# Local attention: own and context keys on two halves of the partitions, three pairs of sum banks, an aligned expert loop

## What is computed

```python
s_win = jnp.einsum('bqhgd,bkhd->bhgqk', qb, kb).astype(jnp.float32) * scale
s_win = jnp.where(valid, s_win, NEG_INF)
s_ctx = jnp.einsum('bqhgd,bkhd->bhgqk', qb, kc).astype(jnp.float32) * scale
...
p = jax.nn.softmax(jnp.concatenate([s_win, s_ctx, s_sink], axis=-1), axis=-1).astype(q.dtype)
```

## Time and profile before

| | |
|---|---|
| median of three executions | 2874.34 us |
| the profiled execution's own time | 2875.95 us |
| its span in the trace | 2874.1 us |
| PE busy | 2626.2 us (91%) |
| DVE busy | 1074.2 us (37%) |
| ACT busy | 706.6 us (25%) |
| granted TensorE clock, mean | 0.964 |

### The profile page before, as it was taken

One profiled execution on the slowest core, in us unless ns is written; L12 is line 12 of the kernel. 1 busy time (PEld: TensorE's weight loads), 2 busy tenths in 40 slices (PEclk: granted clock), 3 DMA queues, 4 the chain that ended last, 5 costly groups with the idle time before them and its releaser, 6 DMA issues. The chain is left out here.

```text
span 2874.1 us, 43176 instructions
## 1 busy us (share of the span) xinstructions
PE 2626.2 (91%) x17318; PEld 1387.9 (48%) x17318; DVE 1074.2 (37%) x2323; ACT 706.6 (25%) x1843; POOL 220.2 (8%) x258
## 2 busy tenths in 40 slices
PE   7999999999998899998799999997899969999987
PEld 3565654564645666655344444435566543332222
DVE  3023341123345665456222121236652562333224
ACT  2134321234322245323111121213342321000000
POOL 1100200000101001012000000001100010000000
PEclk9999999999998999999899999998999979999999
DMA  7244515342714001114899999972102239999996
GB/s 222 81 128 109 155 66 132 103 127 72 186 47 118 8 1 43 66 44 189 331 394 396 399 401 397 403 217 62 28 1 96 96 143 361 410 406 411 411 409 262
DMA packets 268621, 569.96 MB, mean 198 GB/s; under 512 B 12416, under 2 KB 203200, under 8 KB 219328
## 3 DMA queue, kind: packets, MB, share of 16 engines
q1 hardware_dynamic: 256512, 528.69, 50.2%
q0 software_dynamic: 11824, 39.18, 5.0%
q10 hardware_dynamic: 144, 0.14, 0.0%
HBM read 551.53 MB, written 16.42 MB: 198 GB/s over the span
## 5 line engine op out<-in xcount | busy, mean ns | idle before, releaser
L459 PE MATMUL ps<-turned,ring 128*128 128x512 f32 (+1 forms) x1408 | 553.0, 553 | 11.7 <-ACT turned L1605 8.8
L459 PEld LDWEIGHTS ps<-turned,ring 128*128 128x128 f32 x1408 | 271.3, 194 | 282.1 <-issue 262.6
L707 PE MATMUL ps<-ring,mixT 128*128 128x512 f32 x512 | 225.3, 597 | 0.8 <-DVE mixT L1821 0.8
L1260 ACT ACTIVATE work<-ps 128x512 f32<-128x512 f32 x32 | 19.1, 598 | 684.4 <-PE ps L1164 404.5
L505 PE MATMUL ps<-kz,qz 96*128 96x256 f32 (+3 forms) x384 | 164.7, 516 | 23.8 <-DVE qz L2243 8.8
L1849 ACT ACTIVATE probs_v<-ps,col 128x256 f32<-128x256 f32 (+5 forms) x216 | 136.4, 632 | 70.0 <-DVE col L1799 34.7
L1862 ACT ACTIVATE probsT<-ps 128x512 f32<-128x512 f32 (+3 forms) x280 | 120.2, 455 | 134.6 <-PE ps L545 105.9
L707 PEld LDWEIGHTS ps<-ring,mixT 128*128 128x128 f32 x512 | 96.4, 191 | 115.7 <-issue 114.5
L470 PE MATMUL ps<-ring,turned 128*128 128x128 f32 x1216 | 140.3, 278 | 4.5 <-ACT turned L1605 4.5
L1795 DVE TENSOR_REDUCE col<-ps 128x1 f32<-128x256 f32 (+4 forms) x136 | 78.8, 579 | 174.3 <-PE ps L505 168.0
L470 PEld LDWEIGHTS ps<-ring,turned 128*128 128x128 f32 x1216 | 140.0, 195 | 7.9 <-ACT turned L1605 4.8
(11 more groups left out here) (309 smaller groups left out, 3550.3 us busy)
## 6 DMA issues: line engine op xcount, KB each, us to landing
ring<-in_w_gate SPq DMA_DIRECT2D x64, 1024.0 KB, 19.8
mixT<-in_w_up SPq DMA_DIRECT2D x64, 1024.0 KB, 13.5
ring<-in_w_mod SPq DMA_DIRECT2D x96, 512.0 KB, 4.0
ring<-in_w_up SPq DMA_DIRECT2D x48, 1024.0 KB
ring<-in_w_in SPq DMA_DIRECT2D x82, 512.0 KB, 7.2
turned<-in_w_gate SPq DMA_DIRECT2D x32, 1024.0 KB
mixcT<-in_w_down SPq DMA_DIRECT2D x32, 1024.0 KB
probs_v<-in_w_down SPq DMA_DIRECT2D x32, 1024.0 KB
```

The costliest lines, as they stand in the source:

```text
L459: mm = nc.tensor.matmul(ps[:, b, 0:n], w[:, k, :], rhs[:, k, 0:n], start=(k == 0), stop=(k == KD - 1))
L707: mm = nc.tensor.matmul(ps[:, b, :], lhs[:, k, tl * P:(tl + 1) * P], w, start=(k == 0), stop=(k == KD - 1))
```

## The change

- Queries of the window attention are held twice, on partitions 0 to 63 and, by a new ACT copy (`act_queries_twice`, one of 64 x 1024 per query chunk, two per part), on 64 to 127. The window's own keys stay on 0 to 63, its context keys move to 64 to 127 (`act_ctx_keys`, and `act_heads` for `aq` into `QC`). The scores are then a matmul on each half, own keys and all 256 context keys in one; every other score of the second stack (`ca`, `nb`, `cb`) reads 64 partitions instead of 96. PE's first score of a part waits for the copy (`queries_twice`).
- `score_span` places the own scores at the end of the first bank, the context's at the start of the second. POOL's four memsets per layer go.
- `sum_banks` gives layer 0 three pairs of banks, so that only tile 3 waits (for tile 0); the four multiplications of the context's share move on DVE behind the first tile's centring (`dve_gate_context`); `pe_combine_context` waits for tile 2's centring instead of tile 3's.
- PE's expert loop begins at slot 0 of a fetch block.

```diff
--- before.py
+++ after.py
@@ -417,7 +417,15 @@
         def score_span(u):
 
             o = (seq[u] % 2) * 1024 if wide(u[0]) else (seq[u] % 4) * 512
+            if wide(u[0]):
+
+                o += SEQ - (keys_of(u) - NC) * P
             return o, o + keys_of(u) * P
+
+        def score_banks(u):
+
+            o, end = score_span(u)
+            return o // 512 * 512, -(-end // 512) * 512
 
         def probs_span(u):
 
@@ -475,31 +483,33 @@
 
         def pe_scores(pe, u):
             (kind, l, part), t, hh = u
-            w = before(u, score_span)
+            w = before(u, score_banks)
             if w is not None:
 
                 pe.wait_ge(*at("probs", w))
             S = s_psum(u)
-            q = (QC if kind in ("ca", "cb") else qz)[0:KROWS, hh, t * P:(t + 1) * P]
+            q = qz[0:KROWS, hh, t * P:(t + 1) * P]
+            own, other = slice(0, HD), slice(HD, P)
             parts = []
             if kind in ("fox", "mla"):
                 parts = [(q, kz[0:KROWS, hh, 0:(t + 1) * P], 0), (unit16, causal16, t * P)]
             elif kind == "mem":
                 parts = [(q, kz[0:KROWS, hh, 0:CTX], 0)]
             elif kind in ("ca", "cb"):
-                parts = [(q, KC[0:KROWS, part if kind == "ca" else 2 + hh, :], 0)]
+                R, keys = (other, part) if kind == "ca" else (own, 2 + hh)
+                parts = [(QC[R, hh, t * P:(t + 1) * P], KC[R, keys, :], 0)]
             elif kind == "nb":
-                parts = [(q, kz[0:KROWS, hh, :], 0), (q, KC[0:KROWS, 2 + hh, :], SEQ)]
+                parts = [(q[own, :], kz[own, hh, :], 0), (q[own, :], KC[own, 2 + hh, :], SEQ)]
             else:
                 j0, j1 = max(t - 1, 0), min(t + 1, NT - 1)
                 w = (j1 - j0 + 1) * P
-                parts = [(q, kz[0:KROWS, part, j0 * P:(j1 + 1) * P], 0)]
+                parts = [(qz[own, hh, t * P:(t + 1) * P], kz[own, part, j0 * P:(j1 + 1) * P], 0),
+                         (qz[other, hh, t * P:(t + 1) * P], KC[other, part, :], w)]
                 if t > 0:
                     parts.append((unit16, before16, 0))
                 if t < NT - 1:
 
                     parts.append((unit16, causal16, w - P))
-                parts += [(q, KC[0:KROWS, part, c * P:(c + 1) * P], w + c * P) for c in range(NC)]
             for lhs, rhs, o in parts:
 
                 mm = nc.tensor.matmul(S[:, o:o + rhs.shape[-1]], lhs, rhs, start=lhs is not unit16, stop=True,
@@ -945,8 +955,7 @@
                     if l == 0:
                         pe_conv_stat(pe, l, 1, "cvar")
                     q_job(3)
-                pe.wait_ge(*at("roped", (l, "aq", 2 * part + 1)))
-                pe.wait_ge(*at("zero_rows", ("second", l)))
+                pe.wait_ge(*at("queries_twice", (l, 2 * part + 1)))
                 if l == 0:
                     pe.wait_ge(*emptied(("aq", l, 2 * part + 1, 1)))
                 pe.wait_ge(*emptied(("bv", l, 1, 1)))
@@ -1069,9 +1078,11 @@
 
         def pairs_of_rounds(eng, body, first=2, last=EXPERTS - 2):
 
+
+            head = {eng.engine: 0} if eng.engine == mybir.EngineType.PE else None
             for e in range(first):
                 body(e, e % 2)
-            with eng.Fori(first, last, 2) as i:
+            with nc.Fori(first, last, 2, engines=[eng.engine], head_slot=head) as i:
                 body(i, 0)
                 body(i + 1, 1)
             for e in range(last, EXPERTS):
@@ -1095,8 +1106,12 @@
 
         def sum_banks(l, t):
 
-            b = 4 * l + 2 * (t % 2)
+            b = 4 + 2 * (t % 2) if l > 0 else 2 * (t % 3)
             return b, b + 1
+
+        def sums_before(l, t):
+
+            return t - (2 if l > 0 else 3)
 
         def y_gated(l, e):
 
@@ -1134,8 +1149,8 @@
 
                 e = EXPERTS - 1
                 for t in range(NT):
-                    if t >= 2:
-                        pe.wait_ge(*at("dve_step", ("ce", (("experts", l), t - 2))))
+                    if sums_before(l, t) >= 0:
+                        pe.wait_ge(*at("dve_step", ("ce", (("experts", l), sums_before(l, t)))))
                     if l == 0:
                         pe.wait_ge(sem(f"y_landed{t}"), 16)
                     elif t == 0:
@@ -1226,11 +1241,12 @@
             combine_last()
 
             job_ring[:] = [6, 7]
+            if l == 0:
+                pe.wait_ge(sem("y_gated"), 2)
 
         def pe_combine_context(pe):
 
-            pe.wait_ge(sem("y_gated"), 2)
-            pe.wait_ge(*at("dve_step", ("ce", (("experts", 0), NT - 1))))
+            pe.wait_ge(*at("dve_step", ("ce", (("experts", 0), 2))))
             for t in range(NC):
                 for q in range(4):
                     R = slice(32 * q, 32 * q + 32)
@@ -1340,12 +1356,6 @@
                     R = slice(64 * half, 64 * half + 64)
                     ins = nc.vector.tensor_tensor(y_half[l][R, :], grow[R, 0, half * 512:(half + 1) * 512], ps[R, Y, :], ALU.mult)
                 ins.then_inc(sem("y_gated"), 1)
-                if l == 0:
-                    for q in range(4):
-                        R = slice(32 * q, 32 * q + 32)
-                        ins = nc.vector.tensor_tensor(y_quarter[R, :], grow[R, 1, q * 256:(q + 1) * 256],
-                                                      ps[R, YC, 0:256], ALU.mult)
-                    ins.then_inc(sem("y_gated"), 1)
 
             def add_outputs(e):
 
@@ -1714,6 +1724,14 @@
             ins.then_inc(*done("gates", l))
             dve.wait_ge(*at("gates", l))
 
+        def dve_gate_context(dve):
+
+            YC = expert_banks(0)[5]
+            for q in range(4):
+                R = slice(32 * q, 32 * q + 32)
+                ins = nc.vector.tensor_tensor(y_quarter[R, :], grow[R, 1, q * 256:(q + 1) * 256], ps[R, YC, 0:256], ALU.mult)
+            ins.then_inc(sem("y_gated"), 1)
+
         def dve_moe_out(dve, l):
 
             st, nx = ("experts", l), ("pre", l + 1)
@@ -1751,6 +1769,8 @@
                 dve_norm_scale(dve, (nx, t), res(t), xt[:, t % 2, :], final=("tile_ready", (nx, t)))
 
             begin(tiles[0])
+            if l == 0:
+                dve_gate_context(dve)
             for n, t in enumerate(tiles):
                 if last and n + 1 < len(tiles):
                     begin(tiles[n + 1])
@@ -1877,8 +1897,10 @@
             job = (name, l, c, r) if r is not None else (name, l, c)
             n = CTX if r == 1 or name == "memk" else SEQ
             act.wait_ge(*at("job_done", job))
+
+            R = slice(HD, P) if name == "aq" else slice(0, HD)
             for e in range(2):
-                ins = nc.scalar.activation(dst[0:HD, 2 * (c % 2) + e, 0:n], ps[e * HD:(e + 1) * HD, bank_of(job), 0:n],
+                ins = nc.scalar.activation(dst[R, 2 * (c % 2) + e, 0:n], ps[e * HD:(e + 1) * HD, bank_of(job), 0:n],
                                            ACT.Copy, scale=scale)
             ins.then_inc(*done("evac_act", job))
 
@@ -2229,6 +2251,12 @@
             nc.scalar.activation(rt1, ps[:, bank_of(job), :], ACT.Copy,
                                  scale=HD ** -0.5 if name == "aq" else 1.0).then_inc(*done("evac_act", job))
 
+        def act_queries_twice(act, l, c):
+
+            act.wait_ge(*at("roped", (l, "aq", c)))
+            o = 2 * (c % 2)
+            nc.scalar.activation(qz[HD:P, o:o + 2, :], qz[0:HD, o:o + 2, :], ACT.Copy).then_inc(*done("queries_twice", (l, c)))
+
         def dve_rope(dve, l, name, c):
             job = ("rot", l, name, c)
             dve.wait_ge(*at("job_done", job))
@@ -2279,6 +2307,7 @@
             act_rope_in(act, l, "aq", 1)
             if l > 0:
                 act_conv_out(act, l, 0)
+            act_queries_twice(act, l, 0)
             for part in range(2):
                 if part == 1:
                     q_job(2)
@@ -2289,6 +2318,9 @@
                         act_conv_out(act, l, 1)
                 if part == 0 or l == 0:
                     roots_table()
+                if part == 1:
+                    act_queries_twice(act, l, 2)
+                act_queries_twice(act, l, 2 * part + 1)
                 act_softmax(act, ("wa", l, part))
             for c in range(2):
                 act_heads(act, "bk", l, c, 0, kz)
@@ -2344,8 +2376,9 @@
 
         def act_ctx_keys(act, l, job, first):
             act.wait_ge(*at("job_done", job))
+            R = slice(HD, P) if first == 0 else slice(0, HD)
             for e in range(2):
-                ins = nc.scalar.activation(KC[0:HD, first + e, :], ps[e * HD:(e + 1) * HD, bank_of(job), 0:CTX], ACT.Copy)
+                ins = nc.scalar.activation(KC[R, first + e, :], ps[e * HD:(e + 1) * HD, bank_of(job), 0:CTX], ACT.Copy)
             ins.then_inc(*done("evac_act", job))
 
         def dve_second_block(dve, l):
@@ -2574,10 +2607,6 @@
                                    a["mod_rows"][l][w].rearrange("(a p j) r -> p a (j r)", p=P,
                                                                  j=2)).then_inc(sem("modp_landed"), 16)
```

(5 more changed lines are left out.)

## The result

The changed kernel takes 2883.49 us (median of 20 runs, 2875.25 to 2894.37), the kernel before 2872.62 (20 runs). The ratio is 1.003, with an interval of 1.0021 to 1.0038: slower by 0.3%, where 2873.0 was forecast. The profiled execution took 2883.93 us, with a span of 2882.1 and a mean granted clock of 0.957; before it was 0.964. The traces know two levels of that clock, 0.50 and 1.00 ("full"); what lies between is the mean of a window.

A forecast was written before the change was run, and what follows sets the result against it. Bounds: weights' DMA for layer 1's experts, PE for layer 0's experts and window attention, DVE in layer 0's part 0. Terms +0.3 + 2.4 - 2.1 - 3.2 + 2.3 - 1.0 + 0 = -1.3 took 2874.34 to 2873.0 us; range 2861 to 2884.

The forecast's parts named there:

- rival 2: Window attention: the way through the softmax becomes the bound, so PE's gain turns into waiting; 2882 us, chance 0.20.
- the cover of `nb`: Neighbourhood attention: PE's idle 0.53 us per pair, waiting for DVE, covers the division changes; 0.5 us for both phases.
- if PE's idle 0.53 us per pair of `nb` turned into work and more: Neighbourhood attention: a sign, named beforehand, that the prediction would be wrong; 0.53 us per pair.
- The halves (0.52 us per pair): Window attention: context keys run beside own keys, winning 0.52 us per pair of units, 2.6 per part in three parts.
- Rivals 1 and 3: First: division changes nearly free, 2863.5 us, chance 0.30. Second: the array's halves take turns, 2891 us, chance 0.06.
- The opening of a part: Window attention's start at low clock: first to seventh score takes 12.4 us where it took 14.1.
- That the clock rises with time and not with units: Window attention's openings: units five and six fall into the slow stretch, so 0.7 of 2.4 us is given back.
- The copies: ACT's query copies ahead of window-attention parts: 1.05 us each; PE starts 1.1 us late, or 2.2 in layer 1's part 0.
- The combining: End of layer 0's experts: DVE's idle 2.64 us goes, four multiplications of 1.71 us join its chain; -1.0 us.
- The aligned loop (0): Expert loop: it stays loaded without instruction fetches, rounds stay 32.96 us, so alignment changes 0 us.
- That the branch to the new head falls under PE's queued matmuls: PE's expert loop: the branch is hidden behind queued matmuls, within the aligned loop's 0 us.
- Rival 4: Its claim is cut from the text given; counted among the faster outcomes, chance 0.03.

The follow-up runs named there:

- e1: Kernel before, with only the neighbourhood scores changed from 96 rows to the 64 that hold data: 2884.17 us, ratio 1.0039.
- e2: Changed kernel, with the neighbourhood scores back on 96 rows, 32 of them zeroed by POOL: 2872.06 us, ratio 0.9991.
- e6: Changed kernel with 96-row neighbourhood scores, query copies on DVE, and five unread 128x512 products ahead of each window-attention part: 2875.84 us, ratio 1.0002.
- e9: Changed kernel with 96-row neighbourhood scores, query copies on DVE, and two unread 128x512 products ahead of each window-attention part: 2864.32 us, ratio 0.9972.
- e4: Kernel before, with the three pairs of sum banks alone: 2874.38 us, ratio 1.0.
- e8: Kernel before, with the aligned expert loop alone: 2876.26 us, ratio 1.0007.
- e3: Kernel before, with the halves, the query copies and the 64 rows, without the three bank pairs and the aligned loop: 2924.19 us, ratio 1.0176.
- e7: Changed kernel without the aligned loop: 2926.06 us, ratio 1.0173.

## Why the prediction was wrong

The measured time lies in the range by half a microsecond, but the forecast was no difference, and the kernel is slower. That the range holds it is luck: it reached to 2884 for rival 2, which did not come.

- **The step that failed is the cover of `nb`: "In `nb` PE idles for 0.53 us per pair for DVE, which covers it; I take 0.5 us for both phases".** I priced the 64 rows by the time of each matmul, at full clock, and there the cover held (0.22 us left). But the clock was itself a result of these matmuls. On 64 rows it stays low for 17 us at each opening of `nb`; PE is then the bound and the cover is gone. I took 0.5 us; it is 12.3 by the stages and about 11 by e1 and by e2. The prediction named the sign itself ("if PE's idle 0.53 us per pair of `nb` turned into work and more"), and at the openings that is what came. That the prediction used rows with the clock at 0.50 for the openings of `wa`, and left the openings of `nb` as they were, is the gap: every stage whose matmuls change their shape needs its clock asked for again. No rival would have caught it: none had the clock in it.
- **The halves (0.52 us per pair)** held in the main: 0.49 for the pair shown, so 0.145 for a change of division was near. But from the seventh score of layer 1's part 1 to the part's end it is 27.91 us for 29.85, 1.9 us for five pairs, where I had 2.6. Rivals 1 and 3 fall.
- **The opening of a part** held in its form: the third score begins 3.35 us after the first in layer 1's part 1 (3.4 forecast), at 1.38 us per score at the low clock (1.3 forecast). The seventh begins 11.5 us after the first, where 12.4 were forecast and 14.1 were before: 2.6 us won for 1.7. That the clock rises with time and not with units held here: the low stretch of this opening is 10.2 us in both traces, with scores 2.1 and 1.38 us apart. In layer 1's `nb`, on other rows, the stretch went from 3.4 to 17.1 us, so time alone does not set it. That layer 1's part 1 as a whole came out at -4.6 for -4.3 is partly luck, since this error and that of the pairs cancel. With the copies, parts 0 and 1 of layer 1 came out at -1.8 (PE's wait ahead of part 0 grew from 2.87 to 5.10 us, less 4.0) and -3.5 us, for -2.1 and -3.2. Rival 2 is visible only where the clock was forced up (e6, e9).
- **The copies** held: 1.00 us each for 1.05. The fixed part of 0.2 is in the trace of before: ACT's copies of 128, 256, 384 and 512 columns at L2016 take 0.31, 0.42, 0.52 and 0.63 us, 0.107 per 128 columns and 0.20 besides. The the start of layer 0's part 1 came 5.6 us later for 5.7. That part with `ca` gave back 0.9 of it, where I had 2.7; in e2, the same code there, it gave back 3.1. The low stretch was 17.1 us in the one and 10.2 in the other, so this term moves by 2 us with the clock. The 52.64 us of before are themselves short: e1, e4 and e8, with the same code there, take 54.3 to 54.7.
- **The combining** held: -1.1 for -1.0. PE has no wait ahead of tile 3 any more, and DVE none for ACT's root.
- **The aligned loop (0)** was right for the wrong reason. In the kernel before q8 had no packet from 1556 to 1820 us, and that "the loop stays loaded" was read from there; it does not hold in the changed kernel by itself. Without the alignment it costs 42 us (e3, e7), with nine blocks per turn, where the kernel before has none in eight rounds, though branch and body are the same. So whether a turn fetches depends here on something that the alignment changes, and no run here measured for which placings it does. That the branch to the new head falls under PE's queued matmuls held: the rounds of the changed kernel start at 1595.37, 1628.32, 1661.28 and 1694.23 us, 32.95 or 32.96 apart. Rival 4 falls.
- Not explained: +1.5 us in the experts' stretch and +1.5 us in layer 1's projections (3.7 less the 2.2 of the copies); no run was made for them. The trace of before is at the short end in both: e4 and e1 take 675.1 and 675.4 us for its 674.71 in the first, and e1, e4 and e8 0.6 to 1.2 us more in the second.

## What to carry over

When an edit changes the shape of matmuls (rows, columns, division of the array), ask for the granted clock of every stage that it touches, not only for the durations at full clock; a stage whose matmuls are hidden at the full clock can be the bound at 0.50, as `nb` was for 17 us. Zero rows that look like waste (32 of 96 here) were worth more than they cost. And that a loop fetches nothing is not a property of its body: an edit elsewhere took it from no block to nine per turn here (e3), so look at the instruction queue after each edit, or pin the head.

## What the runs showed that I had not expected

- Zeroed rows hold the clock up: scores on 64 instead of 96 rows, with the same output, cost 11 us of 2873 (e1).
- The alignment of one loop is worth 42 us in the changed kernel: without it nine blocks of instructions are fetched and 8.7 us lost in each of five turns (e3, e7).
- Products that nobody reads, put into a wait, raised the clock of what follows from a mean of 0.60 to 1.00 over ten microseconds (e6), but only 1.8 us came of it; at full clock the third score waits for the exponential (e9).
- An execution's time goes with its mean clock: over the 20 runs of the changed kernel it went from 0.961 (2875.25 us) to 0.953 (2894.37).
